# A hybrid attention and state-space layer: sample attention as portions of the attention stage, the next stage's weights made ready there, and quarter turns of the state-space groups on TensorE

## The chip, the cores and the metric

The kernel runs on one core of one Trainium2 chip. The metric is the device time of one execution in microseconds (us); the time before is the median of three executions. All times in traces are microseconds from the span's start.

## What is computed

One layer of a decoder for a prompt of 16 + 4096 tokens and a sample batch of 8 x 8 tokens, all in float32. Attention has 8 query heads of 64 on 2 key heads, a window of 128 keys and one sink for each head; the sample tokens look at 128 cached keys and their own 8. The state space has 32 groups of 16 channels, each with 64 complex states.

```python
def project(x, pos, norm_w, w_in, q_norm_w, k_norm_w):
    z = rmsnorm(x, norm_w) @ w_in          # 1024 columns to 512+128+128+512+512+512
    q, k, v, g_attn, u, g_ssm = jnp.split(z, cuts, axis=-1)
    q, k = rope(rmsnorm(q, q_norm_w), pos), rope(rmsnorm(k, k_norm_w), pos)
...
    s = jnp.einsum('btkgd,bskd->bkgts', qg, kc).astype(jnp.float32) / math.sqrt(HEAD_DIM)
    p = sink_softmax(s, mask[None, None, None], sinks).astype(vc.dtype)
    o = jnp.einsum('bkgts,bskd->btkgd', p, vc)
...
    # ssm_scan: x[l] = lam * x[l-1] + Bbar u[l], complex;  y = Re(C x) + D u
...
    a = rmsnorm(attn_o * jax.nn.silu(g_attn), attn_out_norm_w)
    g = jax.nn.gelu(ssm_y.astype(x.dtype))
    s = g * jax.nn.sigmoid(g @ w_glu + b_glu)
    s = rmsnorm(s * jax.nn.silu(g_ssm), ssm_out_norm_w)
    return x + jnp.concatenate([a, s], axis=-1) @ w_out
```

## The kernel before

The program is five stages, one after the other, each a block of one hand-written program for every engine, with a barrier between them; engines meet through semaphores alone, and within an engine the order is that of the code. SyncE issues the transfers.

**Attention** (`attention_tiles`) goes over 33 tiles of 128 tokens. Products are made in three passes, from a high and a low part of both operands: `high_w` (ScalarE, L901) and `low_w` (VectorE, L1040) split the weights, which come in through four staging slots STG; `high_x` and Pool's L748 split x; `square_x` (ScalarE, L913) sums the squares of x for the reciprocal roots of the norms (VectorE, from L1047). In tile t TensorE does the scores of t, q of t + 1, k and v, the transposes of the probabilities (bank TB), the gate, the values, and the transposes of q, k and gate. ScalarE's exponents are L974, VectorE's row maxima end with the small steps at L1111.

**Sample attention** (`sample_attention`) is a stage of its own for 64 tokens and also makes ready the first weights (L1675 high parts) and inputs of the next stage. **The early stage** (`early_projections`) makes u and the state-space gate, in nine pieces s of 464 tokens: squares L428 (ScalarE), their sum L467 (GpSimd), `total` L480 (TensorE), products L490 to L492. It writes u to memory (scr_u) by channel group.

**The state space** (`state_space`) goes over 32 groups t. A chunk is 16 tokens, a group has 256 of them and one more. VectorE's `vectors(t + 4)` makes powers times input and output columns (WB, WT, CB, CP: L1519 to L1528), GpSimd makes tables of phasors CS (L1330 to L1337) four groups ahead, and in groups 4 to 23 the low parts of the last stage's weights (`low_weight`, L1342). TensorE's `matrices(t)` (L1362 to L1369) makes kernel and transposes, `chunk_inputs` (L1381) two 265-column products, real and imaginary, `outputs` (L1393 to L1406) seven products into y. VectorE's `states` turns the chunk inputs by the phasors (L1536), adds the two halves (L1537), scans (L1538) and turns back (L1542). An imaginary part is had from a real one by SWAP, a matrix that turns by a quarter. SyncE loads U in six transfers a group (L1259) after the outputs of an earlier group, and stores y (L1267).

**The late stage** (`late_projections`) does the half-GLU, the norms and the output projection.

## Time and profile before

| | |
|---|---|
| median of 3 executions | 1922.61 us (1922.33 to 1923.34) |
| profiled execution | 1921.25 us, its span 1919.4 us |
| granted TensorE clock, mean | 0.964 |
| busy | PE 1758.0 us (92%), PEld 1418.5, DVE 1384.1 (72%), ACT 677.3, POOL 533.4 |
| attention, 0 to 730 us | PE busy 680.0 |
| sample attention, 730 to 782.5 | PE busy 22.6 |
| early stage, 782.5 to 1164 | PE busy 374.8 |
| state space, 1164 to 1434 | PE busy 212.2 |
| late stage, 1434 to 1919.4 | PE busy 468.4 |

PE is TensorE's matmuls and PEld its weight loads, DVE is VectorE, ACT ScalarE, POOL GpSimd, SPq the queue of transfers that SyncE issues. A row in order of time has the start, the duration, engine, line, operation, output <- inputs, sizes and, in brackets, how long the engine stood idle before and what ended that. A row by tile has the count and the shortest, median and longest duration in ns. A row by stretch has the stretch, its length, then busy time and count for PE, PEld, DVE, ACT and POOL, then the granted clock, the busy share of the DMA engines and GB/s.

### The profile page before, as it was taken

To read this page: it belongs to the slowest core of one execution; us is meant where nothing else is said; L and a number is where in the kernel's file an instruction comes from. 1 tells how busy PE (TensorE), PEld (TensorE's weight loads), DVE (VectorE), ACT (ScalarE), POOL (GpSimd) and SP (SyncE) were. 2 spreads that over 40 slices of the span, in tenths; PEclk is the share of its full clock that TensorE was granted. 3 is DMA by queue.
4 is the path that set the end of the run, shared out by engine and by line. 5 is a ranking of instruction groups with operands and counts; after the bars stand their busy time and mean duration, and the time that the engine had idled before them with its cause. 6 is when DMAs were issued, how large, how long until landed. Compare 5 with 4: busy or idle time off the path is not lost. (4 is left out here: it accounts for less than half of the span.)

```text
span 1919.4 us, 26075 instructions
## 1 busy us (share of the span) xinstructions
PE 1758.0 (92%) x8731; PEld 1418.5 (74%) x8731; DVE 1384.1 (72%) x3049; ACT 677.3 (35%) x1743; POOL 533.4 (28%) x615
## 2 busy tenths in 40 slices
PE   5899999999999983799999995888868999999999
PEld 4777777777777762688888884666656788888886
DVE  5787887888787874488889945999957456655532
ACT  5444544554454443222223202444424222222210
POOL 1122122222222210322223305889932111111110
PEclk9999999999999995799999997999989999999999
DMA  7112212211211104333143124655447535445331
GB/s 245 54 59 76 70 59 67 78 59 59 86 58 47 42 15 160 81 85 130 60 120 129 50 80 130 153 146 147 119 97 154 144 127 140 127 119 139 108 113 63
DMA packets 200485, 191.69 MB, mean 100 GB/s; under 512 B 121504, under 2 KB 159520, under 8 KB 200352
## 3 DMA queue, kind: packets, MB, share of 16 engines
q1 hardware_dynamic: 191136, 181.63, 31.8%
q10 hardware_dynamic: 9216, 8.39, 2.3%
q8 instruction: 70, 1.15, 0.2%
q14 instruction: 63, 0.52, 0.1%
HBM read 130.88 MB, written 59.10 MB: 99 GB/s over the span
## 5 line engine op out<-in xcount | busy, mean ns | idle before, releaser
L788 PE MATMUL ps_b<-b_WH,b_XH 128*128 128x512 f32 (+1 forms) x792 | 294.8, 372 | 19.4 <-POOL b_XL L748 11.5
L790 PE MATMUL ps_b<-b_WH,b_XL 128*128 128x512 f32 (+1 forms) x792 | 285.1, 360 | 0.0
L789 PE MATMUL ps_b<-b_WL,b_XH 128*128 128x512 f32 (+1 forms) x792 | 285.1, 360 | 0.0
L490 PE MATMUL ps_e<-e_XH,e_WH 128*128 128x464 f32 x576 | 219.9, 382 | 3.4 <-POOL e_ONES L453 3.4
L492 PE MATMUL ps_e<-e_XH,e_WL 128*128 128x464 f32 x576 | 215.7, 375 | 0.0
L491 PE MATMUL ps_e<-e_XL,e_WH 128*128 128x464 f32 x576 | 215.2, 374 | 0.0
L788 PEld LDWEIGHTS ps_b<-b_WH,b_XH 128*128 128x128 f32 x792 | 150.8, 190 | 53.8 <-issue 23.2
L748 POOL TENSOR_TENSOR b_XL<-b_XT,b_XH 128x1024 fp32r<-128x1024 f32 x33 | 79.5, 2410 | 370.1 <-ACT b_XH L908 370.1
L790 PEld LDWEIGHTS ps_b<-b_WH,b_XL 128*128 128x128 f32 x792 | 150.7, 190 | 24.2
L789 PEld LDWEIGHTS ps_b<-b_WL,b_XH 128*128 128x128 f32 x792 | 151.1, 191 | 21.2
L974 ACT ACTIVATE b_SM<-ps_b,b_small 128x128 f32<-128x128 f32 x256 | 113.7, 454 | 110.2 <-DVE b_small L1111 107.6
L490 PEld LDWEIGHTS ps_e<-e_XH,e_WH 128*128 128x128 f32 x576 | 109.0, 189 | 18.3 <-POOL e_ONES L453 3.6
L2012 PE MATMUL ps_l<-W_OUTH,l_AH 128*128 128x512 f32 (+1 forms) x264 | 106.2, 402 | 17.5 <-POOL l_AL L1961 12.9
L2112 DVE SCALAR_TENSOR_TENSOR l_OUT<-ps_l,l_small,l_OUT 128x512 f32<-128x512 f32 (+1 forms) x66 | 48.8, 749 | 100.8 <-PE ps_l L2014 100.8
L491 PEld LDWEIGHTS ps_e<-e_XL,e_WH 128*128 128x128 f32 x576 | 108.9, 189 | 15.1 <-issue 2.0
L492 PEld LDWEIGHTS ps_e<-e_XH,e_WL 128*128 128x128 f32 x576 | 108.8, 189 | 13.8
L1961 POOL TENSOR_TENSOR l_AL<-l_A,l_AH 128x512 fp32r<-128x512 f32 (+1 forms) x33 | 42.4, 1284 | 237.3 <-ACT l_AH L1908 237.3
L2013 PE MATMUL ps_l<-W_OUTL,l_AH 128*128 128x512 f32 (+1 forms) x264 | 104.7, 397 | 0.0
L2014 PE MATMUL ps_l<-W_OUTH,l_AL 128*128 128x512 f32 (+1 forms) x264 | 104.7, 397 | 0.0
L2012 PE MATMUL ps_l<-W_OUTH,l_SH 128*128 128x512 f32 (+1 forms) x264 | 102.9, 390 | 0.0
L2014 PE MATMUL ps_l<-W_OUTH,l_SL 128*128 128x512 f32 (+1 forms) x264 | 102.7, 389 | 0.0
L2013 PE MATMUL ps_l<-W_OUTL,l_SH 128*128 128x512 f32 (+1 forms) x264 | 102.7, 389 | 0.0
(334 smaller groups left out, 3894.6 us busy)
## 6 DMA issues: line engine op xcount, KB each, us to landing
b_XT<-in_xb SPq DMA_DIRECT2D x33, 512.0 KB, 4.0
b_XR<-in_x SPq DMA_DIRECT2D x33, 512.0 KB, 5.1
...
l_X<-in_xr SPq DMA_DIRECT2D x32, 512.0 KB, 4.4
out_out<-l_OUT SPq DMA_DIRECT2D x32, 512.0 KB, 3.0
...
```

Of the source, the lines that this page charges most:

```text
L490: pe.matmul(bank(s, m), WH[:, k, cols], XH[s % 2][:, k, :], start=(k == 0), stop=False)
L491: pe.matmul(bank(s, m), WH[:, k, cols], XL[s % 2][:, k, :], start=False, stop=False)
L492: mm = pe.matmul(bank(s, m), WL[:, k, cols], XH[s % 2][:, k, :], start=False, stop=(k == KD - 1))
L748: pool.tensor_tensor(XL[b][:], XT[b][:], XH[b][:].bitcast(F32), ALU.subtract).then_inc(x_lo, 1)
L788: pe.matmul(bank[:, 0:c1 - c0], XH[b][:, k, :], WH[:, k, c0:c1], start=(k == 0), stop=False)
L789: pe.matmul(bank[:, 0:c1 - c0], XH[b][:, k, :], WL[:, k, c0:c1], start=False, stop=False)
L790: mm = pe.matmul(bank[:, 0:c1 - c0], XL[b][:, k, :], WH[:, k, c0:c1], start=False, stop=(k == KD - 1))
L974: exped.mark(act.activation(SM[:, h, :], scores_of(g)[:, j, t % 2, :], ACT.Exp, bias=NM[:, h:h + 1], scale=RQX[:, h:h + 1], accum_out=SUM[ ...
L2012: pe.matmul(bank, lh, w[0], start=first, stop=False)
L2013: pe.matmul(bank, lh, w[1], start=False, stop=False)
L2014: return pe.matmul(bank, ll, w[0], start=False, stop=last)
L2112: dve.scalar_tensor_tensor(out=o, in0=ps[0:n, 3 + 2 * h, :], scalar=RSS[0:n, i:i + 1], in1=o, op0=ALU.mult, op1=ALU.add).then_inc(o_out, 1)
```

## The change

Sample attention's stage is removed. Its work is cut into portions that stand in attention's tiles 4 to 15, on every engine (`samples(t)`), and share bank TB; the cached keys come already transposed in a constant input. What it made ready for the early stage is made at attention's end, from a new object `Shared` whose five staged weight pieces lie where attention's buffers can spare them; the early stage loads the last three itself. Attention's staging slots go from four to nine, and all squares but the first come after the weights. In the state space TensorE makes the sum of WB's halves, the joining and quarter turn of the turned chunk inputs (`scan_inputs`) and that of the states (`turned_states`), where VectorE added halves and TensorE had a second set of matrices.

```diff
+    def load(self, sp, I, k):
+        if k >= self.STAGED:
+            sp.wait_ge(self.lo, k - self.STAGED + 1)
+        sp.dma_start(self.staged(k), I["w_in"][k * P:(k + 1) * P, C_U:C_U + 2 * DS]).then_inc(self.ld[k % self.STAGED], 16)
+
+    def high(self, act, k):
+        act.wait_ge(self.ld[k % self.STAGED], 16 * (k // self.STAGED + 1))
+        act.activation(self.weights("H", k), self.staged(k), ACT.Copy, scale=self.NW[:, k:k + 1]).then_inc(self.hi, 1)
+
+    def low(self, dve, k):
+        dve.wait_ge(self.hi, k + 1)
+        dve.scalar_tensor_tensor(out=self.weights("L", k), in0=self.staged(k), scalar=self.NW[:, k:k + 1],
+                                 in1=self.weights("H", k).bitcast(F32), op0=ALU.mult, op1=ALU.subtract).then_inc(self.lo, 1)
...
+                for k in range(shared.STAGED, KD):
+                    shared.high(act, k)
...
+                        if m == 0 and s == 0:
+                            pe.wait_ge(shared.lo, k + 1)
...
+        QK_AT, SCORES_AT, MAX_AT, EXP_AT, NORM_AT, CACHED_AT, NEW_AT, GATE_AT, VALUES_AT, SQUARE_AT, TOTAL_AT = 4, (5, 6), 7, 8, 9, 10, 11, 12, 13, 14, 15
...
+                    if t == TOTAL_AT + 2:
+                        sp.wait_ge(s_full, taken(TOTAL_AT))
+                        for k in range(shared.STAGED):
+                            shared.load(sp, I, k)
+                    if t == TOTAL_AT + 4:
+                        sp.wait_ge(tail, 32)
+                        sp.wait_ge(s_st, 16)
+                        for p in range(4):
+                            sp.dma_start(pieces(shared.XT, p), I["xt"][0, :, 2 * p:2 * p + 2, :]).then_inc(nx_ld[p], 16)
...
+                def samples(t):
...
+                    elif t in SCORES_AT:
+                        g = SCORES_AT.index(t)
+                        pe.wait_ge(s_ld, 64)
+                        pe.wait_ge(s_out, taken(t - 1))
+                        for quad in range(2):
+                            for bi in range(4):
+                                b = 4 * quad + bi
+                                q_ = QT0[group(g), b, :, :].rearrange("p j t -> p (j t)")
+                                o = TB[32 * bi:32 * bi + 32, quad * NK:(quad + 1) * NK]
+                                pe.matmul(o[:, 0:P], q_, CKT[group(g), b, :], start=True, stop=True)
+                                mm = pe.matmul(o[:, P:NK], q_, KT0[group(g), :], start=True, stop=True)
+                        mm.then_inc(s_full, 1)
...
+                    elif t == VALUES_AT:
+                        pe.wait_ge(s_out, taken(t - 1))
+                        pe.wait_ge(kept_v, 1)
+                        for b in range(B):
+                            for g in range(NKV):
+                                i, c = 2 * g + b // 4, slice(32 * (b % 4), 32 * (b % 4) + 32)
+                                o = TB[group(g), 32 * b:32 * b + 32]
+                                pe.matmul(o, CV[:, b, group(g)], PTC[:, i, c], start=True, stop=False)
+                                mm = pe.matmul(o, V0[0:NSAMP, group(g)], PTN[0:NSAMP, i, c], start=False, stop=True)
+                        mm.then_inc(s_full, 1)
...
                     if t:
                         scores(t)
+                        samples(t)
...
-                high_w(0)
-                high_w(1)
                 high_x(0)
-                for n in range(2, KD):
+                for n in range(KD + 2):
                     high_w(n)
                 square_x(0)
-                square_x(1)
                 high_x(1)
-                for n in range(KD, 2 * KD):
+                for n in range(KD + 2, 2 * KD):
                     high_w(n)
-                    if n - KD < 3:
-                        square_x(n - KD + 2)
+                for t in range(1, 5):
+                    square_x(t)
...
+                    if t == NT - 1:
+                        act.wait_ge(ga_full, NT)
+                        shared.high(act, 0)
+                        next_high_x(0)
+                        shared.high(act, 1)
...
+                next_high_x(1)
+                shared.high(act, 2)
+                shared.high(act, 3)
+                next_high_x(2)
+                shared.high(act, 4)
+                next_high_x(3)
...
                         rotate(t + 1, 1)
+                    samples(t)
                     if t:
                         split_probs(t)
+                    if t == NT - 1:
+                        for k in range(3):
+                            shared.low(dve, k)
                     if t + 1 < NT:
...
-                dve.wait_ge(a_out, NT - 1)
-                dve.scalar_tensor_tensor(out=VA[:], in0=SA[:], scalar=0.25 / DA, in1=EPSX[:], op0=ALU.mult, op1=ALU.add).then_inc(first, 1)
-                dve.wait_ge(first, 3)
-                rsqrt_chain(dve, ra, Tile(None, 0), RAO[:], VA[:], SA[:], YA[:], 1.0, 0.0)
-                dve.memset(RAO[:, 0:1], 1.0).then_inc(first, 1)
+                dve.wait_ge(nx_hi, 4)
+                dve.tensor_tensor(pieces(NX["L"], 3), pieces(shared.XT, 3), pieces(NX["H"], 3).bitcast(F32), ALU.subtract)
+                for k in range(3, shared.STAGED):
+                    shared.low(dve, k)
...
+                    pe.wait_ge(w_parts, t + 1)
                     if t:
-                        pe.wait_ge(o2_out, t)
+                        pe.wait_ge(w_out, t)
                     for a in range(2):
-                        pe.transpose(psWO[:, P * a:P * a + P], WT[t % RT][:, 8 * a:8 * a + 8, :].rearrange("p t h -> p (t h)"), SWAP[:, 0, :])
-                    mats.mark(pe.matmul(psWO[:, 256:512], SWAP[:, 1, :], c[:, 1:T + 1, :].rearrange("p t h -> p (t h)"), start=True, stop=True))
+                        for i in range(2):
+                            mm = pe.matmul(psW[:, P * a:P * a + P], WB[t % RT][:, i, 8 * a:8 * a + 8, :].rearrange("p t h -> p (t h)"), SWAP[:, 0, :],
+                                           start=(i == 0), stop=(i == 1))
+                    mats.mark(mm)
...
-                    for v in range(2):
-                        for a in range(2):
-                            mm = pe.matmul(psV[t % 2][:, v, 0:NU], W[s][:, a, v, :], U[s][:, a, FROM:FROM + NU], start=(a == 0), stop=(a == 1))
+                    for a in range(2):
+                        mm = pe.matmul(psV[t % 2][:, 0:NU], W[s][:, a, :], U[s][:, a, FROM:FROM + NU], start=(a == 0), stop=(a == 1))
                     mm.then_inc(v_full, 1)
+
+                def scan_inputs(t):
+                    pe.wait_ge(turned, t + 1)
+                    if t:
+                        z_steps.wait(pe, tile(t - 1), 1)
+                    pe.matmul(psZ[:, 0:NC + 1], SWAP[:, 0, :], Z[t % 2][:, 0, :], start=True, stop=False)
+                    pe.matmul(psZ[:, 0:NC + 1], SWAP[:, 1, :], Z[t % 2][:, 1, :], start=False, stop=True).then_inc(z_full, 1)
+
+                def turned_states(t):
+                    s = t % RM
+                    z_steps.wait(pe, tile(t))
+                    pe.wait_ge(h_in, t + 1)
+                    if t:
+                        pe.wait_ge(f_out, t)
+                    pe.matmul(psS[:, 0:NY], SWAP[:, 0, :], CZ[s][:, 0, :], start=True, stop=False)
+                    pe.matmul(psS[:, 0:NC + 1], SWAP[:, 2, :], CZ[s][:, 1, 0:NC + 1], start=False, stop=True).then_inc(st_full, 1)
...
-                    y_full.mark(pe.matmul(y0[:, 0:NC], o2[:, 0:P], CZ[s][:, 1, 0:NC], start=False, stop=True))
...
-                    pe.matmul(y1, o_[:, P:2 * P], c1, start=False, stop=False)
-                    y_full.mark(pe.matmul(y1, o2[:, P:2 * P], CZ[s][:, 1, 0:NC], start=False, stop=True))
...
+                    pe.wait_ge(st_out, t + 1)
+                    y_full.mark(pe.matmul(y0, o_[:, 0:P], st[:], start=False, stop=True))
+                    y_full.mark(pe.matmul(y1, o_[:, P:2 * P], st[:, 0:NC], start=False, stop=True))
...
                 for t in range(G):
+                    turned_states(t)
                     if t + 1 < G:
-                        chunk_inputs(t + 1)
+                        scan_inputs(t + 1)
+                    if t + 2 < G:
+                        chunk_inputs(t + 2)
                     outputs(t)
...
+                def state_copies(t):
+                    act.wait_ge(st_full, t + 1)
+                    if t >= 2:
+                        y_full.wait(act, tile(t - 2))
+                    act.activation(S[t % 2][:], psS[:, 0:NY], ACT.Copy).then_inc(st_out, 1)
+                    act.activation(XS[:, t, 8:9], psS[:, NC:NC + 1], ACT.Copy).then_inc(f_out, 1)
...
-                    wt.link(dve, tile(t), dve.tensor_tensor(WB[:], y_, back, ALU.mult))
                     if t >= RT:
                         mats.wait(dve, tile(t - RT))
-                    wt.link(dve, tile(t), dve.tensor_tensor(WT[t % RT][:], WB[:, 0], WB[:, 1], ALU.add))
+                    dve.tensor_tensor(WB[t % RT][:], y_, back, ALU.mult).then_inc(w_parts, 1)
...
-                    z_steps.link(dve, T_, dve.tensor_tensor(Z[:], psV[t % 2][:, :, 0:n], CS[s][:, :, 0:n], ALU.mult))
-                    z_steps.link(dve, T_, dve.tensor_tensor(Z[:, 0], Z[:, 0], Z[:, 1], ALU.add))
-                    z_steps.link(dve, T_, dve.tensor_tensor_scan(ZS[:], rep_last(PAR[t % RP][:, RHO:RHO + 1], n), Z[:, 0], 0.0, ALU.mult, ALU.add))
...
+                    dve.tensor_tensor(Z[t % 2][:], bcast_mid(psV[t % 2][:, 0:n], 2), CS[t % RC][:, :, 0:n], ALU.mult).then_inc(turned, 1)
...
+                def scan(t):
+                    n = NC + 1
+                    T_ = tile(t)
+                    dve.wait_ge(z_full, t + 1)
+                    z_steps.link(dve, T_, dve.tensor_tensor_scan(ZS[:], rep_last(PAR[t % RP][:, RHO:RHO + 1], n), psZ[:, 0:n], 0.0, ALU.mult, ALU.add))
+                    if t >= RM:
+                        dve.wait_ge(st_full, t - RM + 1)
+                    z_steps.link(dve, T_, dve.tensor_tensor(CZ[t % RM][:, :, 0:n], bcast_mid(ZS[:], 2), CS[t % RC][:, :, 0:n], ALU.mult))
...
                 for t in range(G):
-                    if t + 1 < G:
-                        states(t + 1)
                     if t + 4 < G:
                         vectors(t + 4)
+                    if t + 1 < G:
+                        scan(t + 1)
+                    if t + 2 < G:
+                        turn_inputs(t + 2)
```

VectorE in the state space, one group before: WB and CB are products with powers, WT and CP their sums, Z the turned chunk inputs, ZS the scan, CZ the turned-back states.

```order
L1519 TENSOR_TENSOR g_WB<-g_PAR 128x512
L1522 TENSOR_TENSOR g_WT<-g_WB 128x256
L1525 TENSOR_TENSOR g_CB<-g_PAR 128x544
L1528 TENSOR_TENSOR g_CP<-g_CB 128x272
L1536 TENSOR_TENSOR g_Z<-ps_g,g_CS 128x514
L1537 TENSOR_TENSOR g_Z<-g_Z 128x257
L1538 SCALAR_TENSOR_TENSOR g_ZS<-g_PAR,g_Z 128x257
L1542 TENSOR_TENSOR g_CZ<-g_ZS,g_CS 128x2x257
L1546 SCALAR_TENSOR_TENSOR g_XS<-g_PAR,ps_g 128x8
```

And one group of the change:

```order
L1772 TENSOR_TENSOR g_WB<-g_PAR 128x512
L1775 TENSOR_TENSOR g_CB<-g_PAR 128x544
L1778 TENSOR_TENSOR g_CP<-g_CB 128x272
L1797 SCALAR_TENSOR_TENSOR g_ZS<-g_PAR,ps_g 128x257
L1800 TENSOR_TENSOR g_CZ<-g_ZS,g_CS 128x2x257
L1787 TENSOR_TENSOR g_Z<-ps_g,g_CS 128x514
L1790 SCALAR_TENSOR_TENSOR g_XS<-g_PAR,ps_g 128x8
```

Two additions are gone, the scan reads TensorE's bank, and the turn of the chunk inputs is that of a group later.

TensorE in the state space, one group before, from `matrices(t + 1)` to `outputs(t)`:

```order
L1362 MATMUL ps_g<-g_CP,g_PAR 16x256
L1363 MATMUL ps_g<-g_PAR,g_SWAP 16x16
L1368 MATMUL ps_g<-g_SWAP,g_WT 128x128 x2
L1369 MATMUL ps_g<-g_CP,g_SWAP 128x256
L1381 MATMUL ps_g<-g_U,g_W 128x265 x4
L1393 MATMUL ps_g<-g_U,g_MALL 128x272
L1396 MATMUL ps_g<-g_CZ,g_CP 128x272
L1397 MATMUL ps_g<-g_CZ,g_O 128x256
L1403 MATMUL ps_g<-g_U,g_MALL 128x256
L1404 MATMUL ps_g<-g_U,g_MALL 128x256
L1405 MATMUL ps_g<-g_CZ,g_CP 128x256
L1406 MATMUL ps_g<-g_CZ,g_O 128x256
```

And of the change:

```order
L1612 MATMUL ps_g<-g_CP,g_PAR 16x256
L1613 MATMUL ps_g<-g_PAR,g_SWAP 16x16
L1619 MATMUL ps_g<-g_SWAP,g_WB 128x128 x4
L1648 MATMUL ps_g<-g_CZ,g_SWAP 128x272
L1649 MATMUL ps_g<-g_CZ,g_SWAP 128x257
L1639 MATMUL ps_g<-g_Z,g_SWAP 128x257
L1640 MATMUL ps_g<-g_Z,g_SWAP 128x257
L1632 MATMUL ps_g<-g_U,g_W 128x265 x2
L1659 MATMUL ps_g<-g_U,g_MALL 128x272
L1662 MATMUL ps_g<-g_U,g_MALL 128x256
L1663 MATMUL ps_g<-g_U,g_MALL 128x256
L1665 MATMUL ps_g<-g_S,g_CP 128x272
```

Two products fewer in the outputs (a last row like L1665 follows) and two fewer chunk inputs, against four with SWAP and two more for WB; the chunk inputs are now those of group t + 2.

ScalarE at the end of attention, before: after the gate's copy (GT) come the sums of squares (SQA), the exponents (SM) and the last copies.

```order
L965 ACTIVATE b_GT<-ps_b 128x512
L983 ACTIVATE b_SQA<-b_AT 128x512
L974 ACTIVATE b_SM,b_small<-ps_b,b_small 128x128 x4
L977 ACTIVATE b_small<-b_small 128x4
L974 ACTIVATE b_SM,b_small<-ps_b,b_small 128x128 x4
L977 ACTIVATE b_small<-b_small 128x4
L987 ACTIVATE b_SA<-ps_b 128x1
```

And of the change, where nextH is the next stage's weights and X0H its input:

```order
L1145 ACTIVATE b_GT<-ps_b 128x512
L1193 ACTIVATE b_SQA<-b_AT 128x512
L387 ACTIVATE w_nextH<-w_ST,w_NW 128x1024
L1187 ACTIVATE w_X0H<-w_XT 128x928
L387 ACTIVATE w_nextH<-w_ST,w_NW 128x1024
L1154 ACTIVATE b_SM,b_small<-ps_b,b_small 128x128 x4
L1157 ACTIVATE b_small<-b_small 128x4
L1154 ACTIVATE b_SM,b_small<-ps_b,b_small 128x128 x4
L1157 ACTIVATE b_small<-b_small 128x4
L1197 ACTIVATE w_SA<-ps_b 128x1
L1187 ACTIVATE w_X0H<-w_XT 128x928
L387 ACTIVATE w_nextH<-w_ST,w_NW 128x1024 x2
```

Three pieces stand ahead of the last exponents, and six more behind them.

## Rows read from the trace of the kernel before

**Rows 1.** The busy times by stretch.

```profile
0.00:730.00 730.00, 680.02 (x3753) 527.35 (x3753) 568.49 (x1620) 346.22 (x1019) 152.61 (x201) 0.98 0.21 71
730.00:782.50 52.50, 22.61 (x174) 18.18 (x174) 20.86 (x39) 20.62 (x35) 0.00 (x0) 0.50 0.42 144
1198.40:1412.70 214.30, 181.90 (x853) 138.31 (x852) 204.70 (x279) 94.38 (x351) 190.77 (x244) 0.99 0.56 138
```

**Rows 2.** Order of time, ScalarE and VectorE at the start; the page's loads of XR.

```profile
5.80 1.76 ACT L901 ACTIVATE b_WH<-b_STG,b_NW 128x768 fp32r<-128x768 f32 x2
30.40 1.06 ACT L913 ACTIVATE b_XR<-b_XR 128x1024 f32<-128x1024 f32 x1 [1.67 <-DMA b_XR<-in_x]
...
37.17 0.16 DVE L1047 TENSOR_SCALAR b_MS<-b_SSX 128x5 f32<-128x5 f32 x1
...
b_XR<-in_x SPq DMA_DIRECT2D x33, 512.0 KB, 5.1
```

**Rows 3.** Instructions by tile, sample attention: ns min/median/max, first and last start.

```profile
L1644 PE MATMUL ps_s<-CKT,QTS x32: 387/417/419, 742.5 to 744.7; 64*32 64x128 f32 x32
L1659 PE MATMUL ps_s<-PTC,CV x32: 294/304/314, 761.3 to 772.0; 128*64 128x32 f32 x32
...
L1742 DVE TENSOR_REDUCE small_s<-S_s x1: 953/953/953, 746.2 to 746.2; 128x4 f32<-128x768 f32 x1
```

**Rows 4.** Order of time around the removed stage.

```profile
728.96 0.06 DVE L1173 MEMSET RAO<- 128x1 f32 x1
730.08 0.40 SPq L1611 DMA_DIRECT2D CK<-in_cache_k  x1
...
746.92 1.14 ACT L1675 ACTIVATE e_WH<-STG_s,NW_s 128x1024 fp32r<-128x1024 f32 x1
...
782.86 3.58 ACT L428 ACTIVATE e_XT<-e_XT 128x928 f32<-128x928 f32 x4 [2.84 <-DVEq L541]
...
792.89 0.30 PEld L480 LDWEIGHTS ps_e<-e_ACC,e_ONES 128*128 128x128 f32 x2 [3.38 <-POOL e_ACC L467]
```

**Rows 5.** Order of time, ScalarE before the last exponents of attention.

```profile
711.02 0.46 ACT L974 ACTIVATE b_SM<-ps_b,b_small 128x128 f32<-128x128 f32 x1 [3.14 <-DVE b_small L1111]
```

**Rows 6.** Instructions by tile, VectorE in the state space: ns min/median/max.

```profile
L1522 DVE TENSOR_TENSOR g_WT<-g_WB x32: 424/1372/1479, 1176.0 to 1409.6; 128x256 f32<-128x256 f32 x32
...
L1525 DVE TENSOR_TENSOR g_CB<-g_PAR x32: 724/1027/1741, 1176.8 to 1410.1; 128x544 f32<-128x544 f32 x32
...
L1536 DVE TENSOR_TENSOR g_Z<-ps_g,g_CS x32: 693/694/695, 1190.8 to 1419.7; 128x514 f32<-128x514 f32 x32
L1537 DVE TENSOR_TENSOR g_Z<-g_Z x32: 428/582/924, 1191.5 to 1420.4; 128x257 f32<-128x257 f32 x32
L1538 DVE TENSOR_TENSOR_SCAN g_ZS<-g_PAR,g_Z x32: 695/1099/1105, 1192.5 to 1420.9; 128x257 f32<-128x257 f32 x32
```

**Rows 7.** Order of time, TensorE in one state-space group.

```profile
1302.57 0.61 PE L1362 MATMUL ps_g<-g_CP,g_PAR 128*16 128x256 f32 x2 [1.54 <-DVE g_CP L1528]
1303.25 0.44 PE L1368 MATMUL ps_g<-g_SWAP,g_WT 128*128 128x128 f32 x2
1303.96 1.95 PE L1381 MATMUL ps_g<-g_U,g_W 128*128 128x265 f32 x8
```

**Rows 8.** GpSimd: order of time, and two operations by tile.

```profile
1298.61 1.79 POOL L1342 TENSOR_TENSOR W_OUTL<-g_STG,W_OUTH 128x512 fp32r<-128x512 f32 x1 [0.43 <-ACT W_OUTH L1487]
1306.56 1.79 POOL L1342 TENSOR_TENSOR W_OUTL<-g_STG,W_OUTH 128x512 fp32r<-128x512 f32 x1 [0.42 <-ACT W_OUTH L1487]
...
L1342 POOL TENSOR_TENSOR W_OUTL<-g_STG,W_OUTH x16: 1266/1790/1802, 1259.4 to 1378.2; 128x512 fp32r<-128x512 f32 x16
...
L1335 POOL TENSOR_TENSOR g_CS<-g_CS,g_PB x32: 635/1020/1088, 1180.2 to 1406.8; 128x256 f32<-128x256 f32 x32
```

**Rows 9.** Order of time, SyncE's queue in one group.

```profile
1293.47 3.74 SPq L1259 DMA_DIRECT2D g_U<-scr_u  x6
1297.26 1.69 SPq L1267 DMA_DIRECT2D scr_y<-g_YS  x2
```

568 lines of the change are left out of this document (257 added, 311 removed).

## Prediction

> **What bounds the kernel now.** I read the busy times by stretch first [rows 1]. In attention TensorE works 680 of 730 us at 0.98 of full clock: whatever is added there on TensorE is paid. Between 730 and 782.5 us it works 22.6 us of 52.5 at a granted clock of 0.50, the 1.2 GHz level: this is sample attention, a stage of its own, and a chain of small steps. In the stretch 1198.4 to 1412.7 us (28 groups of the state space, 7.65 us each) VectorE is busy 204.7 of 214.3 us, GpSimd 190.8, TensorE 181.9: VectorE sets the pace and two others are close behind. The first and last microseconds of a stage come from the order of time [rows 2, 4, 5].
>
> **1. The start of attention, -7.5 us.** Nine staging slots replace four, and all squares but one come after the weights. Today ScalarE begins its weight pieces at 5.80 us at 0.88 each, later stands still for inputs (1.67 us before one square), and VectorE begins the first reciprocal roots at 37.17 us, when the last weight piece is split [rows 2]. With inputs early enough ScalarE has work only: eight pieces 768 wide at 0.9 and eight 512 wide at about 0.65 are 12.4 us, two splits of x 2, five squares at 1.15 (1.06 and its read) 5.8, so 20 us from 6 us on. The last squares still take turns in two XR buffers; a load lands a median 5.1 us after its issue [rows 2] and starts when a square frees its buffer, so one or two squares wait: 3 us more, an estimate. So 29.5 us in place of 37.17. Copying q of tile 0 now waits for the squares too, but the tile's rotations need the roots anyhow. Bounds: 0, if the transfers bound it, and -10.
>
> **2. Sample attention within attention, +13 us.** Its TensorE work is added to a TensorE-bound stage. The 32 passes of the scores on cached keys and 32 like them on the new ones went from 742.5 to about 745, the 64 of the values from 761.3 to over 772, all at clock 0.50 [rows 1, 3]. At full clock I take half of each: 1.4 and 5.6; the bounds are half and whole. Seventeen transposes (5 for q and k, 4 each for cached and new probabilities and the gate) at some 0.14 (in [rows 7] a pair and the turned C take 0.71, of which C's 256 columns are some 0.44) are 2.4 us, the total 1 us. The 16 transposes of the cache are gone, since the host lays the cache out. That makes 10.5 us. VectorE's parts stand before split_probs, and its next work ends just ahead of the gate transposes in every tile. In the tiles with no part on TensorE, maxima (0.95 and three small ones, 1.5 us, [rows 3]) and norms (about 1.7 us) should delay TensorE by 1 us each; with the scores 2.5 us. ScalarE's exponents meet idle time. Sum 13 (9 to 20). The waits put in front of q_transposes end earlier: ScalarE or VectorE empties TB while TensorE projects q, k, v and the gate.
>
> **3. The hand-over, -50.8 us.** Attention's last instruction stands at 728.96 us; the early stage's ScalarE begins its squares at 782.86 and its first total on TensorE, which everything behind it waits for, starts at 792.89 [rows 4]. In the new tail ScalarE does two weight pieces and one x piece ahead of the last exponents: 1.14 + 0.9 + 1.14 = 3.2 us (x at a quarter of 3.58) in an idle stretch of 3.14 [rows 4, 5]. Three low parts of weights on VectorE, some 1.2 each, fit between its last probabilities and the last gating, while TensorE computes the values, late by half a microsecond at most (an estimate). Two more follow and take the place of the root chain that ends the stage today (14 small instructions, 3 us at 0.16 and more each [rows 2]): end at about 727. From the last instruction to the next stage's first transfer pass 1.1 us (730.08), so the early stage begins at 728.2. There ScalarE first does three weight pieces (3.4 us), then the four squares, and GpSimd's additions end 9 us after the first square: 728.2 + 3.4 + 1.0 + 9.0 = 741.6, plus 0.5 for TensorE's colder start, against 792.89. The root chain moves into s = 4 of the early stage, 3 us on VectorE; I cost it at nothing, because projections run up to six banks ahead there. Without that cover: 3.
>
> **4. The state-space groups, -22.5 us.** VectorE loses the addition that makes WT (1.37) and the one that joins Z (0.58), with their gaps of 0.04 [rows 6]. GpSimd's rows give the present period, 1306.56 - 1298.61 = 7.95 [rows 8]; so VectorE needs 5.93. The scan now reads TensorE's bank in place of Z. Z's own product, one operand in PSUM, takes 693 to 695 ns in all 32 groups, while the addition with both operands in SBUF takes 428 to 924: only the latter are held up by GpSimd. If the scan behaves as Z does, it goes from 1.10 to its minimum 0.70 and VectorE needs 5.5. But WT's 1.37 against 0.42 alone is mostly the split of the weights that GpSimd does at that time; CB stands there next, its maximum is 1.74 against 1.03. So up to 0.9 comes back: 5.9 to 6.8.
>
> By "SBUF — State Buffer", section "Who interferes with whom", of the Trainium skill, a VectorE instruction with two SBUF inputs and a GpSimd instruction that reads SBUF exclude each other for a whole instruction, and one with a single SBUF input does not contend. The trace agrees for Z. By that rule the scan is freed; without it VectorE keeps its 0.4 us, and TensorE still sets the pace, so the sum is the same within 2 us.
>
> TensorE: one group takes 7.95 - 1.54 waiting, less some 0.1 of drain, = 6.3: K and D 0.68, transposes and turned C 0.71, four chunk inputs in eight passes 1.79 (1.95 less the drain), so seven outputs 3.1, 0.44 each [rows 7]. New: 0.68; four real products of 128 columns instead of two transposes, eight passes at half a chunk-input pass, 0.9 (1.1 at the transposes' pace); two chunk inputs 0.9; four turning products 1.77; five outputs 2.2. That is 6.45 (to 6.65): TensorE is no lighter and becomes the bound.
>
> GpSimd: phasors 5.74 (7.95 - 1.79 - 0.42 waiting) and the weight split 1.79, in 20 of the 32 groups. Alone the split takes 1.27, and one of the additions 0.64 against a median of 1.02 [rows 8]. Two or three of seven contending instructions of VectorE go, which gives back about 0.8: 6.7 with weights, under 5.5 without. Since its tables run four groups ahead, part of the excess is absorbed. SyncE issues six loads in 3.74 and two stores in 1.69 [rows 9], with parameters and weights 6.2. Four queues within 0.5 us of each other don't interlock perfectly: I take 6.8 with weights and 6.55 without. Of the 28 groups 20 carry weights: 20 x 6.8 + 8 x 6.55 = 188.4, against 214.3: -25.9. The pipeline is one step deeper (two turned inputs and a scan before the first group): +4; the last groups lose 0.6. Bounds of the stage: -8 (7.4 with weights) and -30 (6.45 throughout). ScalarE loses four copies and gains one of 272 columns: no stretch of it fills.
>
> Sum: -7.5 + 13 - 50.8 - 22.5 = -67.8. The profiled execution took 1921.25 us (span 1919.4), 1.4 under the median of three, 1922.61. So 1853.5 by the profile, 1855 as a median. The late stage is unchanged.
>
> **Rivals.**
> - *The state space gains little.* GpSimd gets nothing back, or SyncE's queue sets the pace: groups stay at 7.5 and 7.0. For it: GpSimd's 7.53 busy of 7.95. Against: its durations fall wherever VectorE rests. The stage then gives 4 us: 1873. Chance 0.13.
> - *Everything at its floor*: 6.45 in each group, samples 9 us. 1843. Chance 0.12.
> - *The parts in attention cost twice as much*, 26 us, because each holds its engine's queue while TB is waited for: 1868. For it: VectorE has hardly any slack in a tile. Against: every part's inputs were made a tile earlier. Chance 0.1.
> - *Slower than before.* chunk_inputs(t + 2) needs U one group earlier than chunk_inputs(t + 1) did. The loads of U start after the outputs of a group and 3.74 us of issue lie ahead [rows 9]; with 0.4 for parameters there remain about 5.5 us to land at a period of 6.6. Two periods are about 7.3 us plus the landing, so the whole gain of 68 us is lost at a period of 9.1, a landing of 11 us. Nothing in the trace lands so late: DMA engines are 0.56 busy [rows 1]. Chance 0.02: 1930.
> - *No change*, each gain eaten by a wait: 0.01. The forecast itself: 0.62, with its own range 1846 to 1864.
>
> The range 1843 to 1874 takes in the first two rivals and the third. A measurement of this kernel can tell 0.2%, 4 us. Faster 0.97, same 0.01, slower 0.02.
>
> **What would show it.** The early stage's first total near 793 - 7.5 + 13 - 51 = 747 us. The first roots near 29.5. Groups 6.5 to 6.9 us apart, TensorE over 95% busy there, the scan at 0.70 and CB the slowest of VectorE. Tiles 5 to 15 longer by 13 us in all, most of it in tile 13. I am wrong if TensorE waits before chunk inputs (U late) or before scan inputs (VectorE late), if GpSimd shows no idle time in all groups at over 7.3 us a group, or if the early stage starts later because of the last weights.

## The result

The changed kernel takes 1875.43 us (median of 4, 1871.62 to 1875.93) against 1922.47: a ratio of 0.9752 (0.9735 to 0.9769). It is faster by 47 us, not by 67; the prediction's range ended at 1874. In the profiled executions (spans 1919.4 and 1874.1) the difference of 45.3 us is measured from the landmarks that the prediction used:

| stretch | predicted | measured |
|---|---|---|
| start to the keys' transposes of tile 0 (47.04, now 43.69) | -7.5 | -3.35 |
| from there to those of tile 32 (658.87, now 679.70) | +13 | +20.83 |
| to the early stage's first total (86.98, now 41.07) | -50.8 | -45.91 |
| to the last product of the early stage (368.60, now 370.45) | 0 | +1.85 |
| to the first product of the late stage (277.45, now 258.30) | -22.5 | -19.15 |
| to the end (480.46, now 480.89) | 0 | +0.43 |

All six terms came out worse than forecast, the last by less than half a microsecond. Of the kernel after, busy times by stretch: attention, the early stage, sixteen state-space groups, one group alone.

```profile
0.00:748.70 748.70, 693.42 (x3906) 541.85 (x3906) 585.32 (x1627) 361.19 (x1044) 162.59 (x204) 0.97 0.23 79
750.70:1135.00 384.30, 377.52 (x1746) 331.62 (x1746) 308.21 (x699) 92.83 (x114) 89.18 (x65) 0.98 0.30 93
1182.30:1288.40 106.10, 106.10 (x545) 83.14 (x544) 95.09 (x127) 51.44 (x172) 95.58 (x130) 1.00 0.64 163
1288.40:1300.00 11.60, 8.61 (x36) 6.22 (x36) 8.96 (x13) 3.62 (x13) 11.28 (x18) 0.85 0.59 151
```

In the third row TensorE is busy all 106.1 us: 6.63 us a group, with weights and without, where [rows 1] had 7.65 and VectorE as the bound. VectorE by tile, which answers to [rows 6]:

```profile
L1797 DVE TENSOR_TENSOR_SCAN g_ZS<-g_PAR,ps_g x32: 691/692/692, 1166.3 to 1374.9; 128x257 f32<-128x257 f32 x32
...
L1775 DVE TENSOR_TENSOR g_CB<-g_PAR x32: 711/1140/1250, 1149.8 to 1354.0; 128x544 f32<-128x544 f32 x32
```

The scan takes 0.69 in every group, as the prediction had it from Z's rows.

**The stretched tiles.** The keys' transposes stand 20.7 us apart, but 23.25, 25.0 and 25.3 ahead of tiles 8, 9 and 10 and 30.9 ahead of 14. Order of time, VectorE, then GpSimd, in those three tiles:

```profile
199.38 2.27 DVE L1364 TENSOR_TENSOR b_s_small<-b_s_small 128x4 f32<-128x4 f32 x1
...
221.34 0.43 DVE L1286 TENSOR_TENSOR b_ZS<-b_RAW,b_TAB 128x256 f32<-128x256 f32 x1 [1.21 <-ACT b_RAW L1100]
...
223.61 2.46 DVE L1287 TENSOR_TENSOR b_ZS<-b_RAW,b_TAB 128x64 f32<-128x64 f32 x1
...
249.08 3.40 DVE L1375 TENSOR_SCALAR w_ST<-w_ST,b_s_small 128x192 f32<-128x192 f32 x4
...
199.23 2.40 POOL L870 TENSOR_TENSOR b_XL<-b_XT,b_XH 128x1024 fp32r<-128x1024 f32 x1 [10.57 <-ACT b_XH L1088]
223.58 2.40 POOL L870 TENSOR_TENSOR b_XL<-b_XT,b_XH 128x1024 fp32r<-128x1024 f32 x1 [11.17 <-ACT b_XH L1088]
249.52 2.40 POOL L870 TENSOR_TENSOR b_XL<-b_XT,b_XH 128x1024 fp32r<-128x1024 f32 x1 [12.16 <-ACT b_XH L1088]
```

A maximum of four columns takes 2.27 us (0.16 in the kernel before), a product of 64 columns 2.46 (others 0.22), four norms 3.40 together (1.38 before): each while GpSimd subtracts. The product of 64 columns is none of the samples' parts. It stands there late because ScalarE did the samples' exponents first (1.85 us from 218.82 on) and VectorE waited 1.21 us for the copy of q behind them, the first row of that tile. TensorE pays at the end of the tile, and then once more:

```profile
229.59 1.08 PE L1016 MATMUL ps_b<-b_PC,b_VS 128*64 128x512 f32 x4 [2.43 <-DVE b_PP L1349]
...
233.24 0.33 PE L1032 MATMUL ps_b<-b_ID,b_RK 128*128 128x128 f32 x1 [1.12 <-DVE b_RK L1301]
...
234.66 3.68 PE L949 MATMUL ps_b<-b_KT,b_QT 64*128 64x256 f32 x16
```

The scores of L949 take 3.68 us in place of 2.00: the granted clock falls to 0.50, by stretch:

```profile
232.00:235.00 3.00, 1.45 (x9) 0.93 (x9) 2.34 (x8) 1.22 (x3) 0.00 (x0) 0.96 0.00 0
235.00:238.00 3.00, 3.00 (x16) 2.48 (x14) 0.00 (x0) 0.77 (x2) 1.36 (x3) 0.50 0.76 225
```

Ahead of the fall TensorE worked 1.45 of 3.0 us. At which of the tiles 9 and 10 the clock falls differs from run to run, and so do their lengths (see the experiments).

**The tile of the values.** Busy times by stretch from its first sample product (324.51) on:

```profile
324.50:330.20 5.70, 5.70 (x52) 4.72 (x50) 4.78 (x13) 3.48 (x16) 0.71 (x2) 1.00 0.48 188
330.20:332.60 2.40, 2.40 (x16) 1.97 (x15) 1.03 (x3) 0.43 (x3) 0.00 (x0) 0.53 0.02 7
332.60:335.00 2.40, 2.40 (x8) 1.85 (x7) 0.00 (x0) 0.00 (x0) 0.00 (x0) 0.50 0.00 0
```

TensorE is busy all the time, yet after 5.7 us of products of 32 columns the clock falls to 0.5, the 1.2 GHz level, until about 337. So the tile pays 8.2 us of passes (64, the first 50 of them 0.115 apart at full clock, not the 0.09 that I took, the rest 0.175) and some 2 us of slow projection.

**The hand-over and the one long group.** Order of time at attention's end, then around the group that starts at 1288.4:

```profile
737.56 5.56 DVE L391 SCALAR_TENSOR_TENSOR w_nextL<-w_ST,w_NW,w_nextH 128x1024 fp32r<-128x1024 f32 x3
743.05 0.68 DVE L1387 TENSOR_TENSOR b_AT<-ps_b,b_GT 128x512 f32<-128x512 f32 x1
...
743.75 0.33 SPq L854 DMA_DIRECT2D scr_a<-b_AT  x1
...
1282.58 4.46 SPq L1523 DMA_DIRECT2D scr_ys<-g_YSS  x8
...
1295.01 1.13 PE L1632 MATMUL ps_g<-g_U,g_W 128*128 128x265 f32 x4 [2.99 <-issue]
```

And the wait of SyncE at attention's end (total, times, longest us):

```profile
SPq L858 <- DMA scr_a<-b_AT: 5.2, 1, 5.2
```

Three low parts take 5.56 us ahead of the last gating (one is 3.18 us long, the others 1.27), and its output then needs 5.5 us to land (2.0 before), behind three loads. In the state space eight stores fill SyncE's queue in group 16, and TensorE waits 3.0 us before chunk inputs.

### The profile page after: what moved, and what is told of

It reads as the page before. It is cut to its first block and busy times, and to the rows that moved or that the text cites. A ratio compares the mean times of both kernels' runs of the same rounds, so it can differ in the third digit from the quotient of the medians.

```text
span 1874.1 us, 26223 instructions
## 1 busy us (share of the span) xinstructions
PE 1759.9 (94%) x8822; PEld 1428.2 (76%) x8822; DVE 1341.9 (72%) x2969; ACT 666.1 (36%) x1668; POOL 527.0 (28%) x618
## 5 line engine op out<-in xcount | busy, mean ns | idle before, releaser
L559 PE MATMUL ps_e<-w_X0H,w_nextH 128*128 128x464 f32 x320 | 123.7, 386 | 2.5 <-POOL e_ONES L518 2.5
L2066 PE MATMUL ps_l<-W_OUTH,l_AH 128*128 128x512 f32 (+1 forms) x264 | 106.7, 404 | 17.8 <-POOL l_AL L2015 13.1
L561 PE MATMUL ps_e<-w_X0H,w_nextL 128*128 128x464 f32 x320 | 121.2, 379 | 0.0
L560 PE MATMUL ps_e<-w_X0L,w_nextH 128*128 128x464 f32 x320 | 121.0, 378 | 0.0
L1962 ACT ACTIVATE l_AH<-l_A 128x512 fp32r<-128x512 f32 (+1 forms) x33 | 20.5, 622 | 228.9 <-DMA l_A<-scr_a 228.9
L498 ACT ACTIVATE e_TH<-e_TG 128x464 f32<-128x464 f32 x36 | 20.8, 592 | 224.8 <-DVE e_TG L603 224.8
L2158 DVE SCALAR_TENSOR_TENSOR l_OUT<-ps_l,RAO,l_X 128x512 f32<-128x512 f32 (+1 forms) x66 | 48.4, 748 | 72.8 <-DMA out_out<-l_OUT 51.3
```

The lines of the kernel that those rows point to most:

```text
L559: pe.matmul(bank(s, m), high, XH[s % 2][:, k, :], start=(k == 0), stop=False)
L560: pe.matmul(bank(s, m), high, XL[s % 2][:, k, :], start=False, stop=False)
L561: mm = pe.matmul(bank(s, m), low, XH[s % 2][:, k, :], start=False, stop=(k == KD - 1))
L2066: pe.matmul(bank, lh, w[0], start=first, stop=False)
```

## The experiments

Each starts from the changed kernel, unless said, and is timed against the kernel before. "Tiles 8, 9, 10" are the distances above. The changed kernel's own ratio is 0.9735 to 0.9769, and of the runs that start from it only 3 and 14 have an interval wholly below that; in the others the distances of the profiled execution have to decide. These vary too. In the eight runs that edit nothing in those tiles (5, 6, 8 to 13), tile 8 is 23.24 to 23.30, but tile 9 is 22.44 to 25.41 and tile 10 23.29 to 25.32; with the changed kernel's own, the three together are 69.3 to 73.6 us, 71.9 in the mean.

**1. Sample parts into idle time.** VectorE's maxima and norms move behind the gating, ScalarE's exponents ahead of the tanh.

```diff
                         rotate(t + 1, 1)
-                    samples(t)
+                    if t not in (MAX_AT, NORM_AT):
+                        samples(t)
...
                         gate_attn(t)
+                    if t in (MAX_AT, NORM_AT):
+                        samples(t)
```

> The changed kernel with VectorE's maxima and norms of the samples (tiles 7 and 9 of the loop) put behind the gating, at the tile's end, where VectorE stands idle for 2.2 to 2.8 us, and ScalarE's exponents (tile 8) put where it waits 3.0 us before the tanh. Theory A: the three stretched tiles (the keys' transposes 23.3, 25.0 and 25.3 us apart, against 20.7) come from VectorE's and ScalarE's parts standing ahead of work that TensorE waits for, lengthened by one hold of GpSimd each. Then these tiles fall to 20.7 to 21.5, and the time by 9 to 11 us, to 1864 to 1867. Theory B: the stretch is TensorE's own (the samples' products and waits for bank TB): the tiles stay as they are, 1875.

1870.03 us (ratio 0.9711 to 0.9746). Tiles 20.47, 24.76, 20.85: two of three as theory A says, one not. There GpSimd's subtraction was met by another instruction, since the maxima stood ahead of a chain of roots:

```profile
222.52 2.31 DVE L1289 TENSOR_TENSOR b_ZS<-b_RAW,b_TAB 128x64 f32<-128x64 f32 x1
...
221.98 2.77 POOL L870 TENSOR_TENSOR b_XL<-b_XT,b_XH 128x1024 fp32r<-128x1024 f32 x1 [10.73 <-ACT b_XH L1088]
```

**2. The same parts one place later only.**

```diff
                     if t:
                         split_probs(t)
+                    if t in (MAX_AT, NORM_AT):
+                        samples(t)
```

> The changed kernel with VectorE's maxima and norms moved by one place only, behind the split of the probabilities; they still stand ahead of the roots, the keys and the gate that TensorE waits for. Theory A1, the time is VectorE's work as such (1.5 us of maxima, 1.8 us of norms): tiles of 23.3 and 25.3 us stay, since that work is still ahead; at most 0.5 us is saved. Theory A2, most of it is GpSimd's 2.4 us subtraction holding a VectorE instruction that reads SBUF twice (2.27 us for a maximum of 4 columns, 3.40 for norms that took 1.38 in the kernel before): the split reads TensorE's bank and isn't held, so the parts come when GpSimd is through, and the two tiles lose 1.5 to 2 us each: 1871 to 1872.

1874.78 us (0.9736 to 0.9765), tiles 21.29, 24.99, 23.79, then 22.84. Tile 8 lost 1.96 us as A2 says. Tile 10 lies within its spread and tile 11 is 1.6 us longer, all of it at the lower clock (mean 0.93, which is 1.6 us of 22.84), so for the norms nothing is gained or shown. By the time alone the run is unclear.

**3. All parts from the maxima on one tile later as well**, away from the roots.

```diff
-        ... VALUES_AT, SQUARE_AT, TOTAL_AT = 4, (5, 6), 7, 8, 9, 10, 11, 12, 13, 14, 15
+        ... VALUES_AT, SQUARE_AT, TOTAL_AT = 4, (5, 6), 8, 9, 10, 11, 12, 13, 14, 15, 16
```

> The changed kernel with VectorE's sample parts behind the gating and ScalarE's ahead of the tanh, as in the run that ended at 1870, and all parts from the maxima on one tile later. In that run two of three tiles shrank (20.5 and 20.9 us) and one stayed at 24.8: there the maxima stood in the tile whose end also has the chain of reciprocal roots (every fourth), the work behind came 1.5 us late, and the rotation's last products met GpSimd's 2.77 us subtraction (2.31 us for one of 0.22). Theory A, a VectorE part costs nothing in idle time and some 4 us once lateness carries a two-input instruction into GpSimd's: no tile is over 21.6 before the tile of the values, 11 us less than the changed kernel: 1864. Theory B, ScalarE's exponents make that tile long wherever they are: one tile of 24 to 25 stays, 1868 to 1870.

1863.01 us (0.9685 to 0.9712). Tiles 8 to 14 take 20.46 to 20.87: the same VectorE and ScalarE work costs nothing there. Theory A, and here the time shows it too: 12.4 us less than the changed kernel.

**4. GpSimd's subtraction cut short** in the three tiles, all else in place; the kernel leaves out seven eighths of the low parts of x there.

```diff
-                    pool.tensor_tensor(XL[b][:], XT[b][:], XH[b][:].bitcast(F32), ALU.subtract).then_inc(x_lo, 1)
+                    n = 1 if t in (9, 10, 11) else KD
+                    pool.tensor_tensor(XL[b][:, 0:n], XT[b][:, 0:n], XH[b][:, 0:n].bitcast(F32), ALU.subtract).then_inc(x_lo, 1)
```

> The changed kernel with GpSimd's subtraction that makes the low part of x cut to an eighth for tiles 9, 10 and 11 (the other seven eighths keep an older tile's values, so the outputs of these tiles are off; the place, the order and all of VectorE's and TensorE's work are as they were). Theory A: in each of the three stretched tiles one VectorE instruction with two inputs in SBUF is held for as long as that 2.4 us subtraction runs (2.27 us for a maximum of 4 columns, 2.46 for a product of 64, 3.40 for norms of 1.38), and this is 6 to 7 of the 11.2 us; with 0.3 us to hold them the tiles take 21.2, 22.7 or less and 22 to 23.3 in place of 23.25, 25.0 and 25.3: 6 to 9 us less, 1867 to 1869. Theory B: VectorE is late by its own work: under 1 us less, 1874 to 1875.

1870.20 us (0.9711 to 0.9744); tiles 21.33, 23.05, 23.37, together 5.8 us less than in the changed kernel's profile and 4.1 less than in the mean of the nine. VectorE by tile, here:

```profile
L1365 DVE TENSOR_TENSOR b_s_small<-b_s_small x1: 361/361/361, 200.4 to 200.4; 128x4 f32<-128x4 f32 x1
...
L1376 DVE TENSOR_SCALAR w_ST<-w_ST,b_s_small x4: 314/418/524, 246.3 to 247.2; 128x192 f32<-128x192 f32 x4
```

The maximum takes 0.36 in place of 2.27, the norms at most 0.52 each. Tile 8 lies clear of its spread, by 1.9 us: that is GpSimd's hold. Tile 9's 2.0 us are shown by another comparison: in experiments 6 and 13, which edit nothing there, the product of 64 columns happened to miss the subtraction (0.22 us), and the tile took 22.71 and 22.44 us where the seven others with the hold took 24.98 to 25.41. Tile 10 depends on where the clock falls: in tile 10 itself, as here, the unedited runs take 24.93 to 25.33 there, and 23.29 to 23.64 where it falls in tile 9. So GpSimd's hold is 4 to 6 us, up to half, of the 11.3 us that the three tiles had over those of before; the rest is the parts' own time, the wait for ScalarE and slow clock (1.6 to 1.8 us), and how it divides isn't shown.

**5. Values in four tiles**, a quarter of the products in each.

```diff
-                        for b in range(B):
+                        q = VALUES_AT.index(t)        # VALUES_AT is (13, 14, 15, 16)
+                        for b in range(2 * q, 2 * q + 2):
```

> The changed kernel with the samples' values in four tiles, 16 passes each, in place of 64 in one; same products. Theory A (the clock's part of the 10.2 us is from the 6 to 8 us of narrow passes in a row): each of four tiles is longer by 1.9 us and the granted clock stays at 1.00, together 7.5 where it was 10.2: 2.7 us less, 1872.5. Theory B (the passes themselves cost it all, the clock fell for another reason): 10.2 us over four tiles, 1875. Theory C: each extra hold of bank TB makes TensorE wait, over 0.5 us a tile: 1877 or more.

1871.49 us (0.9719 to 0.9748). The four tiles are 22.52, 22.30, 22.29, 22.29: 6.5 us over four tiles of before, against 10.2 in one. The clock stays:

```profile
323.90:325.80 1.90, 1.90 (x19) 1.53 (x17) 1.68 (x4) 0.00 (x0) 0.75 (x2) 1.00 0.87 325
325.80:331.00 5.20, 5.20 (x25) 4.30 (x24) 3.86 (x13) 3.92 (x18) 0.00 (x0) 1.00 0.22 90
```

The same products in pieces keep the clock, theory A; it fell only where all 64 passes stood in a row.

**6. Values of the new keys merged**, 2 products of 256 columns for 16 of 32.

```diff
-                                pe.matmul(o, CV[:, b, group(g)], PTC[:, i, c], start=True, stop=False)
-                                mm = pe.matmul(o, V0[0:NSAMP, group(g)], PTN[0:NSAMP, i, c], start=False, stop=True)
+                            pe.matmul(TB[group(g), 0:256], V0[0:NSAMP, group(g)], PTN[0:NSAMP, 2 * g:2 * g + 2, :]..., start=True, stop=False)
+                            for b in range(B): ... pe.matmul(TB[group(g), 32 * b:32 * b + 32], CV[:, b, group(g)], PTC[:, i, c], start=False, ...)
```

> The changed kernel with the samples' products on their new values as 2 of 256 columns in place of 16 of 32, so 18 products where there were 32 (same result). The tile of the values now takes 30.9 us, 10.2 more than its neighbours. Theory A: 8.3 us are the passes, 0.115 us each at full clock whatever their 32 columns, and 2 us more the granted clock, which fell to the 1.2 GHz level from 330 us on after 6 us of such passes and stayed for 7 us. With 16 x 0.23 + 2 x 0.44 = 4.6 us of passes and no fall the tile takes 25.3, 5.6 less: 1869.5. Theory B: the clock falls anyway, and only 3.7 us are saved: 1871.5.

1867.44 us (0.9691 to 0.9736). The tile takes 23.93: 7.0 us less, more than the 5.6 expected; the clock is 1.00 there. The 18 products take 3.2 us and not 4.6, since their narrow passes are cheaper than I took:

```profile
319.12 1.12 PE L995 MATMUL ps_b<-w_ST 128*64 128x32 f32 x16
```

Sixteen passes of 32 columns start 0.066 us apart here, where passes on the cached and on the new keys (128*64 and 64*64) took turns at 0.115. So the 0.115 is not the price of 32 columns. Whether the turns between the two shapes or those between the two key heads cost it, no run separates.

**7. The state-space change alone**, in the kernel before.

> The kernel before with the state space of the changed kernel and nothing else of the change. By the two traces the stretch from the last product of the early stage to the first of the late one fell from 277.5 to 258.3 us. If that is the state-space edit's own worth, it gives 19.2 us here too: 1903. If part of it came from the other edits (what lies in memory and queues when the stage begins), this gives 15 us or less: 1907 and above. The prediction's term was 22.5: 1900. One stretched group, 11.6 us in place of 6.6, should be seen here too if it is the state space's own queue.

1902.89 us (0.9885 to 0.9916): 19.4 us by the medians, 16 to 22 by the interval, which agrees with the 19.15 in the whole. In its profile the stage's stretch is 16.4 us shorter (277.45, now 261.03), with the long group at 13.02 us.

**8. to 10. The long group.** The eight stores of group 16 spread over groups 16 to 23 on SyncE; on ScalarE; and all at the stage's end.

```diff
-                    if t == 16:
-                        store_samples(0)
+                    if 16 <= t < 24:                      # on SyncE, the first
+                        store_samples(0, (t - 16,))
...
+                    if 16 <= t < 24:                      # on ScalarE, the second
+                        act.dma_start(scr["ys"][0:256, 8 * i:8 * i + 8]..., YSS[SG * i:SG * i + SG, 0:16, :]).then_inc(out_st, 16)
...
                 store_y(G - 1)
+                store_samples(0)                          # the third
                 store_samples(1)
```

> The changed kernel with the eight transfers that store half of the samples' outputs spread over groups 16 to 23, one a group, in place of all eight in group 16. In the trace SyncE spends 4.46 us on these eight issues and 1.3 on a weight's, so the loads of U of the next group start 5 us late, and TensorE waits 3.0 us for chunk inputs and then works 4 us at the 1.2 GHz level: one group takes 11.55 us, 4.9 more than the others' 6.63. Theory A: with the issues spread that group takes 6.6, so 4.9 us less, 1870. Theory B: the stall is from something else at that place (weights, parameters): it stays, 1875.

> The changed kernel with the eight stores of the samples' outputs issued by ScalarE, one a group from 16 on, and none by SyncE there. Spread on SyncE's queue they made six groups 7.1 to 7.7 us long in place of one of 11.55, each with TensorE waiting before its chunk inputs. Theory A, SyncE's queue is full (the loads of U, two stores, weights and parameters take 6.2 of 6.63 us), and U comes as late as the queue is long: without these issues all groups take 6.63, 4.9 us less, 1870. Theory B, the stores' small packets hold the DMA engines and so U, whoever issues them: groups of 7 us and over stay, 1875. ScalarE has the time: it is busy half of a group.

> The changed kernel with all sixteen stores of the samples' outputs at the end of the state space, none in group 16. Theory A: the issues on SyncE's queue made U late in group 16, and spread on either queue, their small packets made it late too; with nothing of them in the middle all groups from the fourth on take 6.63 us, 4.9 us less, and the end has 8 more issues of 0.56 us, 4.5 us if nothing hides them: 1870.5 to 1875. Theory B: the stall is not theirs: one group of 9 us or more stays, and the end is longer: 1879.

1875.30 (0.9738 to 0.9780), 1876.93 (0.9742 to 0.9773) and 1875.59 (0.9744 to 0.9773): no gain in any. On SyncE six groups of 7.08 to 7.70 us replace the one; on ScalarE two of 7.08 and 8.28. At the end no group from the fourth on is over 6.79, so the stores did make the long group; but the stretch from the stage's last product to the first late one grows from 13.5 to 17.8 us, which takes the gain back. On ScalarE the groups did save 2.9 us in the profile (first to last output product, 204.36, now 201.49), which speaks for SyncE's queue, theory A, in that part. But the stage's start, from the last early product to the first output product, was 42.58 us in place of 38.42. It was 41.09 and 41.38 in experiments 11 and 5 too, which don't touch the state space, and no run tests why. So by the times nothing was gained; that the 4.9 us can't be had is not shown.

**11. The low parts behind the last gating.**

```diff
-                    if t == NT - 1:
-                        for k in range(3):
-                            shared.low(dve, k)
...
-                for k in range(3, shared.STAGED):
+                for k in range(shared.STAGED):
```

> The changed kernel with VectorE's first three low parts of the next weights behind the last gating of attention in place of ahead of it. They take 5.56 us, and the gating comes 3.4 us later than it would by the kernel before. Theory A: VectorE's work sets the end of the stage in any order (gating 0.7, one low part of x 1.1, five low parts of 1.3 to 1.85 each): behind the gating it ends 8.3 to 11 us later, at 0 to 1.5 us later than now: 1875 to 1876.5. Theory B: the chain from the gating over ScalarE's squares, GpSimd's additions and TensorE's total to the last copy sets the end; it starts 3.4 us earlier, so 3 us are saved: 1872.

1880.11 us (0.9764 to 0.9800): 5 us more than the changed kernel, with intervals that just touch, and neither theory. The profiled execution has a granted clock of 0.956 in the mean, where the others that start from the changed kernel have 0.968 and more, so its distances are a little long as well. The next stage's first product stands 31.3 us behind the keys of tile 32, in place of 27.6. Order of time on SyncE:

```profile
750.35 0.33 SPq L383 DMA_DIRECT2D w_ST<-in_w_in  x1
750.72 0.43 SPq L854 DMA_DIRECT2D scr_a<-b_AT  x1
...
757.42 0.33 SPq L165 DMA_DIRECT2D A<-in_ssm_a  x1
```

The last load waits for a staging slot that a low part frees, and the stage's last store stands behind it in the queue: its tile was gated at 745.1 and the store is issued at 750.72. SyncE then waits 4.8 us for the landing.

**12. That store ahead of the loads.**

```diff
-                for k in range(shared.STAGED, KD):
-                    shared.load(sp, I, k)
                 sp.wait_ge(gated, last)
                 sp.dma_start(scr["a"][last * P:(last + 1) * P, :], AT[last % 2][:]...)
+                for k in range(shared.STAGED, KD):
+                    shared.load(sp, I, k)
```

> The changed kernel with the store of attention's last tile issued ahead of the last three loads of the next weights. In the trace that store takes 5.5 us to land, behind three loads of 512 KB, against 2.0 us in the kernel before, and SyncE waits 5.2 us for it at the end of the stage. Theory A: the store's landing ends the stage; issued at 743.8 it lands at 746, and ScalarE's last copy (748.7) ends the stage in its place: the next begins 0.9 us earlier, at 749.8, 1874. Theory B: the loads are now the later ones, and the next stage's first high parts wait for them: 0 to 1 us longer, 1875 to 1876.

1872.06 us (0.9727 to 0.9754). The wait for the landing falls from 5.2 to 0.4 us, and the 27.6 us to 26.76: 0.84 less, as theory A has it, and too little for the time alone to show.

**13. Tile 0's own root.**

```diff
-                for t in range(1, 5):
-                    square_x(t)
...
                 tanh(0)
+                for t in range(1, 5):
+                    square_x(t)
...
-    return 0 if t < 5 else (t - 5) // 4 + 1
+    return (t + 3) // 4
```

> The changed kernel with the first reciprocal root taken for tile 0 alone, as soon as its own square is there; those of tiles 1 to 4 follow, and ScalarE's squares of tiles 1 to 4 stand behind tile 0's tanh. Now the roots begin at 33.8 us, when the square of tile 4 is made, 7 us after VectorE's last weight part, and DMA engines are 0.90 busy (327 GB/s) from 5 to 33 us. Theory A: the transfers of the x rows for the squares hold the start: tile 0's keys are transposed 4 to 7 us earlier (now 43.7), and the time falls by as much, 1869 to 1871. Theory B: the weights' transfers and tile 1's own inputs hold it, so tile 0 is earlier and tile 1 waits: 0 to 1.5 us.

1873.77 us (0.9730 to 0.9768). Keys of tile 0 at 36.39 in place of 43.69, but those of tile 3 only 1.3 us earlier: the x rows' transfers held tile 0, and the next tiles take back what it gains. Theory B in the sum.

**14. Five edits together** (3, 6, 13, ScalarE's stores, 12).

> The changed kernel with five edits together: the sample parts as in the run of this call that moves them, the new values' products merged (7.0 us less in that tile), tile 0's own root, ScalarE's stores of the samples' outputs, and attention's last store ahead of the loads. If they add up: 11 + 7.0 + 1.3 + 4.9 + 0.9 = 25 us under the changed kernel, 1850. If the two edits of the state space's queue and of the stage's end bring nothing: 1856. Over 1862 would say that the tiles' edits share one cause and do not add.

1851.19 us (ratio 0.9615 to 0.9641), 1.3% below the changed kernel's ratio and near the 1850 of parts that add up. By the profile the gain is attention's: the keys of tile 32 stand at 702.99 in place of 723.39. The state-space stretch is 257.71 us: ScalarE's stores left one group of 7.23 and none longer, 4.4 us less from the first output product to the last, and its start was 42.00 us long in place of 38.42. The tiles up to 14 take at most 20.9 us from the eighth on, that of the values 23.7.

## Why the prediction was wrong

**The start.** I let ScalarE set it and gave the transfers 3 us. The time after shows them as the bound: ScalarE stands still 2.58 and 1.87 us before its last two squares, while the DMA engines are busy 0.90 (327 GB/s) from 5 to 33 us, and the roots start at 33.8 and not 29.5. By stretch, ScalarE, then VectorE at the first roots:

```profile
5.00:33.00 28.00, 17.34 (x72) 13.47 (x72) 15.82 (x17) 20.04 (x28) 8.05 (x6) 0.95 0.90 327
...
32.62 1.06 ACT L1093 ACTIVATE b_XR<-b_XR 128x1024 f32<-128x1024 f32 x1 [1.87 <-DMA b_XR<-in_x]
...
33.80 0.17 DVE L1266 TENSOR_SCALAR b_MS<-b_SSX 128x5 f32<-128x5 f32 x1 [6.99 <-ACT b_XR L1093]
```

The lower bound named the case (0, if the transfers bound it); the value chosen was too near the other end.

**Samples in attention: the step that failed.** "Sum 13": up to tile 14 they cost 22.9 us, of which tiles 17 to 32 gave 2.2 back, for a reason that I did not test. Three entries of the sum were wrong. The first is "I take half of each" for the values' time at half clock: their tile cost 10.0 us more than before and not 5.6, since the passes took 0.115 us each, two thirds of their time at 0.50, and the clock fell behind them (experiments 5 and 6). The second is "should delay TensorE by 1 us each": the tiles of the maxima and the norms took 2.6 and 4.4 us more. I had added VectorE's durations as [rows 3] show them. They come from a stage where GpSimd was idle ([rows 1], 0.00 busy) and were 2.0 to 2.1 us longer where they met its subtraction (4). The third is "ScalarE's exponents meet idle time", a term of nothing: that tile took 4.3 us more, since the exponents made VectorE 1.2 us late and the lateness carried one of its products into GpSimd's subtraction. Against that, all other tiles up to the 13th were together 1.6 us longer, where the sum leaves some 5 for them, so that the miss of the term, 7.8 us, is smaller than those of its entries: in part luck. The rival "cost twice as much" had about the size, 26 us, but not the cause: no wait for bank TB shows. The rule that I used for the state space, from "SBUF — State Buffer", section "Who interferes with whom", of the Trainium skill (a VectorE instruction with two inputs in SBUF and a GpSimd one that reads it shut each other out), should have been held against every VectorE instruction that the change moved. The trace agrees with it here: 2.27 us against 0.36 for the same maximum, with GpSimd's subtraction at 2.40 and 0.46.

**The hand-over.** The place was right, 4.9 us of 50.8 were missing. The three low parts took 5.56 us and not 3.6, one of them 3.18 us beside GpSimd (2.98 us of subtraction at 737.87), so TensorE's last output was gated 3.4 us late in place of half a microsecond. And the end of a stage was taken from the last computing instruction; the transfer behind it ended later (11 and 12).

**The state space.** TensorE as the new bound, the freed scan and the 6.45 to 6.8 us a group were right: 6.63. What I put down as the unlikely rival, U late since it is needed a group earlier, is real in one group of 28, where SyncE has eight more issues. I had added its queue to 6.2 us of 6.6 and left the stores of group 16 out: 4.9 us. A second miss is the stage's start, from the last early product to the first output product: 31.87 us before and 38.42 after, 6.6 more where I had put 4 for the deeper pipeline. Groups of 6.63 in place of the 6.8 and 6.55 that I took gave 2.8 back, which is luck in the sum: I had charged for queues that get in each other's way, and the steady groups show nothing of it. The sum of a queue has to include what comes once.

**The sum** was 1853.5 for the profiled execution and 1875.9 came: 7.8 us from the tiles, 4.9 from the hand-over, 4.2 from the start, 3.4 from the state space, 2.3 from the rest. Of the rest, 1.3 us stand in the first piece of the early stage (from the first total to the second 29.03 us, 27.76 before, at a granted clock of 0.89 against 0.94), and the root chain that I had costed at nothing in s = 4 did cost under 0.1 (42.51 us, 42.43 before). The errors had one sign. Most terms were costed at their undisturbed time; that this is why all of them missed to one side is my reading, and the steady groups are the exception.
